# A one-core transformer layer with retrieved experts: the blocks of gate matrices are moved to the end of the first expert pass, the last eight activations stay on chip, gates are read back eight chunks at a time

## What is computed

```python
def peer_block(tok, wq, keys, u, v):
    p = tok.shape[0]
    qr = (tok @ wq).reshape(p, PEER_HEADS, 2, PEER_DQ // 2).astype(jnp.float32)
    s = jnp.einsum('phcd,hckd->phck', qr, keys.astype(jnp.float32))
    top_s, top_i = lax.top_k(s, PEER_TOPK)
    cand = top_s[:, :, 0, :, None] + top_s[:, :, 1, None, :]
    ids = top_i[:, :, 0, :, None] * N_KEYS + top_i[:, :, 1, None, :]
    best, j = lax.top_k(cand.reshape(p, PEER_HEADS, PEER_TOPK * PEER_TOPK), PEER_TOPK)
    eidx = jnp.take_along_axis(ids.reshape(p, PEER_HEADS, PEER_TOPK * PEER_TOPK), j, axis=-1)
    g = jax.nn.softmax(best, axis=-1)
    act = jax.nn.gelu(jnp.einsum('phkd,pd->phk', u[eidx], tok))
    return jnp.einsum('phk,phkd->pd', (g * act).astype(tok.dtype), v[eidx])
```

## Time and profile before

| | us |
|---|---|
| median of 3 runs | 1929.91 (1926.39 to 1932.4) |
| profiled execution, its own time | 1931.49 |
| its span (first to last instruction) | 1929.8 |
| PE busy in the span | 1827.1 (95%) |
| DVE busy in the span | 1566.1 (81%) |

### The profile page before, as it was taken

One profiled execution on the slowest core, in us unless ns is written; L12 is line 12 of the kernel. 1 busy time (PEld: TensorE's weight loads), 2 busy tenths in 40 slices (PEclk: granted clock), 3 DMA queues, 4 the chain that ended last, 5 costly groups with the idle time before them and its releaser, 6 DMA issues.

```text
span 1929.8 us, 34458 instructions
## 1 busy us (share of the span) xinstructions
PE 1827.1 (95%) x12531; PEld 1206.1 (62%) x12542; DVE 1566.1 (81%) x2939; ACT 860.4 (45%) x1310; POOL 1068.1 (55%) x671
## 2 busy tenths in 40 slices
PE   9999999999998989999978999998999999999996
PEld 7647777777777756566545666664555555555554
DVE  7975566455357589999979999995699999999997
ACT  6444446565445534333435666662333333333331
POOL 2732122222245748667688888888455555555551
PEclk9999999999999989999999999999999999999998
DMA  5732114223354545678799999999999999999993
GB/s 204 217 106 91 55 56 122 97 76 107 134 171 156 183 151 166 211 239 289 269 387 343 405 414 416 415 378 405 377 399 401 401 402 402 393 400 396 400 363 131
DMA packets 178077, 517.61 MB, mean 268 GB/s; under 512 B 19032, under 2 KB 61024, under 8 KB 177448
## 3 DMA queue, kind: packets, MB, share of 16 engines
q1 hardware_dynamic: 85280, 246.22, 35.3%
q0 software_dynamic: 55296, 201.35, 27.2%
q10 hardware_dynamic: 37384, 68.50, 9.8%
HBM read 458.55 MB, written 57.46 MB: 267 GB/s over the span
## 4 chain that ended last, share of the span: by engine, by line
PE 39%; DVE 26%; DMA 23%; issue 4%; POOL 4%; ACT 3%; ACTq 1%; SPq 0%; DVEq 0%; POOLq 0%
DMA raw<-in_v_units 21%; PE ps L1942 17%; PE ps L2061 10%; DVE rows L1699 4%; PE ps L1958 3%; DVE w_lo L1828 2%; POOL w_lo L601 2%; ACT w_hi L725 2%; DMA rows<-in_u_rows,rowi 2%; PE ps L2215 2%; POOL rows L627 1%; DVE accS L1848 1%; DVE hot L1808 1%; DVE hot_hi L1811 1%; PE ps L2195 1%
## 5 line engine op out<-in xcount | busy, mean ns | idle before, releaser
L601 POOL TENSOR_TENSOR w_lo<-raw,w_hi 128x1024 bf16<-128x1024 f32 x253 | 554.7, 2200 | 489.6 <-ACT w_hi L725 450.7
L725 ACT ACTIVATE w_hi<-raw 128x1024 bf16<-128x1024 f32 x381 | 400.2, 1053 | 452.1 <-DMA raw<-in_v_units 274.5
L660 POOL DMA_INDIRECT rows<-in_v_units,rowi x192 | 290.9, 1515 | 238.3 <-DVE accS L1848 190.0
L1942 PE MATMUL ps<-h_hi,w_hi 128*128 128x384 bf16 x1024 | 337.8, 330 | 17.7 <-ACT hb L1119 17.7
L2444 PE MATMUL ps<-W_hi,w_hi 128*128 128x384 bf16 x992 | 324.9, 327 | 21.4 <-DVE W_lo L1866 19.6
L1942 PE MATMUL ps<-h_lo,w_hi 128*128 128x384 bf16 x1024 | 337.6, 330 | 0.0
L1942 PE MATMUL ps<-h_hi,w_lo 128*128 128x384 bf16 x1024 | 337.3, 329 | 0.0
L2444 PE MATMUL ps<-W_hi,w_lo 128*128 128x384 bf16 x992 | 324.3, 327 | 0.0
L2444 PE MATMUL ps<-W_lo,w_hi 128*128 128x384 bf16 x992 | 324.2, 327 | 0.0
L1699 DVE CUSTOM_DVE_ANT_0 rows<-rows,ps 128x1024 f32<-128x1024 f32 x192 | 227.5, 1214 | 39.6 <-DMA rows<-in_u_rows,rowi 38.4
L627 POOL DMA_INDIRECT rows<-in_u_rows,rowi x192 | 201.7, 1051 | 98.0 <-DVE dots L1699 52.9
(11 more groups left out here) (469 smaller groups left out, 3415.1 us busy)
## 6 DMA issues: line engine op xcount, KB each, us to landing
raw<-in_u_units SPq DMA_DIRECT2D x128, 512.0 KB, 5.5
raw<-in_v_units SPq DMA_DIRECT2D x128, 512.0 KB, 12.3
raw<-in_units SPq DMA_DIRECT2D x123, 512.0 KB, 3.2
hd<-hb ACTq DMA_DIRECT2D x128, 192.0 KB, 6.2
Hb<-hd SPq DMA_DIRECT2D x32, 768.0 KB, 11.2
gd<-gsb ACTq DMA_DIRECT2D x48, 384.0 KB, 9.4
Gb<-gd SPq DMA_DIRECT2D x32, 576.0 KB, 8.4
gz<-stage ACTq DMA_DIRECT2D x24, 288.0 KB, 2.1
```

What stands on the lines that cost most here:

```text
L601: pool.tensor_tensor(w_lo[:, k % RING, :], raw[:, k % RAW, :], w_hi[:, k % RING, :], ALU.subtract).then_inc(lo_ready, 1)
L660: pool.indirect_dma_start(out=rows[:, (ND + n) % RG, :], out_offset=None, in_=table, in_offset=bass.IndirectOffsetOnAxis(ap=index, axis=0))\
L725: act.activation(w_hi[:, k % RING, :], raw[:, k % RAW, :], ACT.Copy).then_inc(hi_ready, 1)
L1942: last = pe.matmul(ps[:, bank + half, 0:n], w[:, slot, col:col + P], x(k)[:, half * n:(half + 1) * n], start=(k == 0 and w is w_hi and x i ...
```

## The change

- **Gate blocks** start at body 8 (`J_G` = 8) and end with the first half; no plain bodies follow.
- **Dots** move: 11 instead of 6 per `pairs_of`, and between its steps; 6 before the exponentials, 12 before the turned routes (74 in all before the first gate step, before it was 60). The other 118 all lie in the 48 gate steps, 2 or 3 in each; before, 2 in each (6 in one), and 32 after the last.
- **Last activations**: body 15 writes its GELU results straight into `Hb`, with no store and no read; the second half starts with those eight chunks and then takes chunks 0 to 119.
- **Gates by eights**: `Gb` holds 8 chunks; SP reads 1152 KB for every second group, in pieces of 1536 bytes instead of 768.
- **First group's `w_out`**: its eight tiles use eight PSUM banks instead of two, so PE no longer waits there for the residual add (`x2_ready`); three `w_lo` move from POOL to DVE (`low_a`); the load of the keys is issued earlier.
- Smaller: the copy into `share` goes (the normalising multiply writes it); `accS`, `eq3`, `Gb` and `Hb` lie elsewhere, so one wait of the first sum goes.

```diff
-J_G = 6
+J_G = 8
+LOW_A = {5: U_WQ + 2, 6: U_WQ + 4, 7: U_WQ + 6}
-DOTS_EARLY = 6
-DOTS_WAIT, DOTS_HELD = 24, 4
-X_TURN = 32
-DOTS_TWO = 4
+DOT_STEPS = (1, 2, 3, 4, 5, 6, 9, 12, 15, 16, 19)
+DOTS_EARLY = len(DOT_STEPS)
+DOTS_EXP, DOTS_WAIT = 6, 12
+X_TURN = 22
+GG = 2 * GRP
+LAST_ON = NCH - BODY
...
+DOTS_BEFORE = DOTS_WQ + NFT * DOTS_EARLY + DOTS_EXP + DOTS_WAIT
+def dots_until(i):
+    if i <= X_TURN:
+        return DOTS_BEFORE + (NST - DOTS_BEFORE) * i // X_TURN
+    return NST + NX * (i - X_TURN) // (N_STEP - X_TURN)
...
+            def load_group(g, pg, gates=None):
+                sp.wait_ge(w_mul, (g - 1) * GRP)
                 sp.dma_start(Hb[pg][:, :, :].rearrange("e c t -> e (c t)"),
-                             hd[bass.ds(g, 1)].rearrange("o e c t -> (o e) (c t)")).then_inc(gh_in[pg], 16)
+                             hd[bass.ds(g - 2, 1)].rearrange("o e c t -> (o e) (c t)")).then_inc(h_in[pg], 16)
+                if gates is not None:
+                    load_g(*gates)
...
+            for k in range(RAW):
+                load(a["v_units"][LAST_ON + k], (U_V + k) % RAW, False, U_V + k - RAW + 1)
+            sp.wait_ge(paired, 1)
             for b in range(2):
                 sp.wait_ge(b_written[b], NBK // 2 * PIECES * 16)
+            load_g(NCH // GG - 1, 0)
+            for k in range(RAW, BODY):
+                load(a["v_units"][LAST_ON + k], (U_V + k) % RAW, False, U_V + k - RAW + 1)
+            sp.wait_ge(unit_used, U_V)
+            load_g(0, 1)
...
-            def chunk(j, k, first=False):
+            def chunk(j, k, first=False, keep=False):
                 act.wait_ge(unit_used, j * BODY + (U_PEER + k + 1))
+                if keep:
+                    act.activation(Hb[k // GRP][:, k % GRP, :], ps[:, k % 2, 0:TD], ACT.Gelu_apprx_tanh).then_inc(gelu_done, 1)
+                    high_half(None, U_PEER + k, j * 32 + 16 * ((U_PEER + RING + k) // RAW + 1))
+                    return
...
-            for j in range(J_END, NCH // BODY - 1):
-                for k in range(BODY):
-                    chunk(j, k)
-            for k in range(BODY):
-                chunk(NCH // BODY - 1, k)
-                for p in FIRST_W.get(k, ()):
-                    w_high(2 * p, 2 * p)
             act.wait_ge(dot_done, ND)
             act.activation(acts[:, :], dots[:, :], ACT.Gelu_apprx_tanh).then_inc(acts_done, 1)
+            w_high(0, 0)
+            w_high(2, 2)
             w_high(GRP, GRP)
...
-                dve.tensor_tensor(xT[:, j, TD:T], ps[:, j % 2, 0:NA], xT[:, j, TD:T], ALU.add).then_inc(x2_ready, 1)
+                dve.tensor_tensor(xT[:, j, TD:T], ps[:, j, 0:NA], xT[:, j, TD:T], ALU.add).then_inc(x2_ready, 1)
...
+                if j in LOW_A:
+                    low_a(LOW_A[j])
...
-            for s in range(dots_until(N_STEP), ND):
-                dot(s)
...
-                if j >= 2:
-                    pe.wait_ge(x2_ready, j - 1)
```

More of the change, by code:

```diff
@@ L228, in row_chunk @@
     if d < NFT * DOTS_EARLY:
[L229 to L237, removed]
+        return 5 + d * 42 // (NFT * DOTS_EARLY)
+    if s - RG < DOTS_BEFORE:
+        return 48 + (d - NFT * DOTS_EARLY) * 2 // 3
+    i = min(x for x in range(N_STEP) if s - RG < dots_until(x + 1))
+    return J_G * BODY - 1 + i * BODY // G_BODY
 def acc_slot(j):
@@ L382, in program @@
         assert used[0] <= ACT_HI + 2 * KT * T * 2
-        accS = place("accS", ACT_HI, [P, D], F32)
         used[0] = ARENA
@@ L413, in program @@
         tripB = sb("tripB", [P, 3, TD], F32)
+        eq3 = place("eq3", used[0], [P, 2, TOPK, HP], BF16)
+        eq = sb("eq", [P, 2, TOPK, P], BF16)
+        iota16 = sb("iota16", [P, TOPK, P], BF16)
         pair = sb("pair", [P, 4, TD], BF16)
@@ L445, in program @@
         wb = [sb(f"wb{p}", [P, 2, TD], F32) for p in range(2)]
-        Gb = [sb(f"Gb{b}", [P, NBK, GRP, TBLK], F32) for b in range(2)]
-        Hb = [sb(f"Hb{b}", [P, GRP, TD], F32) for b in range(2)]
+        accS = sb("accS", [P, D], F32)
+        assert NBK * GG * TBLK * 4 <= 2 * KT * TD * 2 and 2 * KT * TD * 2 + GRP * TD * 4 <= 2 * KT * T * 2
+        assert FREED + (NBK * GG * TBLK + GRP * TD) * 4 <= FREED + 3 * TD * 4 + 2 * TOPK * P * 2 + TOPK * P * 2
         assert used[0] <= TOP
@@ L537, in _, with load_g @@
                     load(a["u_units"][i * RAW + k], (U_PEER + k) % RAW, False, i * RAW + (U_PEER + k - RAW + 1))
[L538 to L542, removed]
+            def load_g(s, b):
+                sp.dma_start(Gb[b][:, :, :, :].rearrange("e b c t -> e b (c t)"),
+                             gd[:, :, bass.ds(s * GG, GG), :].rearrange("b e c t -> e b (c t)")).then_inc(g_in[b], 16)
@@ L555, in _ @@
-            for b in range(2):
[L556 to L565, removed]
@@ L566, in _ @@
-            for b in range(2):
-                sp.wait_ge(h_written[b], 8 * NCH)
+            load_g(NCH // GG - 1, 0)
[3 more added lines that the diff above has]
+            load_g(0, 1)
+            for b in range(2):
+                sp.wait_ge(h_written[b], 8 * LAST_ON)
+            with sp.Fori(0, (NG - 4) // 4) as i:
+                for b in range(4):
+                    load_group(i * 4 + (2 + b), b % 2, (i * 2 + (1 + b // 2), b // 2) if b % 2 else None)
@@ L634, in _ @@
                 low_half(n, n)
-            with pool.Fori(1, U_OUT2 // RING) as i:
+            with pool.Fori(1, U_WQ // RING) as i:
                 for k in range(RING):
                     low_half(i * RING + k, k)
-            for n in range(U_OUT2 // RING * RING, U_PEER + RING):
+            for n in range(U_WQ // RING * RING, U_PEER + RING):
+                if n in LOW_A.values():
+                    continue
+                if n - 1 in LOW_A.values():
+                    pool.wait_ge(lo_ready, n)
                 low_half(n, n)
@@ L1043, in _ @@
                 high_unit(U_OUT + j + RING)
+                if j == 1:
+                    act.dma_start(keys[:, :, :], a["keysT"]).then_inc(keys_in, 16)
                 if j:
@@ L1135, in two_bodies @@
                     for k in range(BODY):
-                        chunk(it * 2 + (J_G + b), k)
+                        chunk(it * 2 + (J_G + b), k, keep=last and b == 1)
                         if first and b == 0 and k == 1:
@@ L1586, in _, with low_a @@
                 merged_low(j)
+            def low_a(n):
+                dve.wait_ge(hi_ready, n + 1)
+                dve.wait_ge(lo_ready, n)
+                dve.tensor_tensor(w_lo[:, n % RING, :], raw[:, n % RAW, :], w_hi[:, n % RING, :],
+                                  ALU.subtract).then_inc(lo_ready, 1)
             def out_low_a(k):
@@ L1757, in _ @@
                     pairs_of(i, NPH, top[:, i - 1, :, :], topi[:, i - 1, :, :], topf, abf, eq, iota16,
-                             tripB[:, :, (i - 2) * P:(i - 1) * P])
-                for x in range(DOTS_EARLY):
-                    dot(DOTS_WQ + (i - 1) * DOTS_EARLY + x)
+                             tripB[:, :, (i - 2) * P:(i - 1) * P], dot_beside)
             EARLY_DONE = DOTS_WQ + NFT * DOTS_EARLY
+            for x in range(DOTS_EXP):
+                dot(EARLY_DONE + x)
             NB_ = (NFT - 1) * NPH
@@ L2429, in _ @@
             two_bodies(NBLK // 2 - 1, last=True)
-            with pe.Fori(J_END, NCH // BODY) as j:
-                for k in range(BODY):
-                    chunk(j, k)
             pe.wait_ge(b_evac, N_STEP)
```

53 lines of the change are left out of this document (24 added, 29 removed).

## The result

| | before | after |
|---|---|---|
| median of 8 runs each, us | 1929.82 | 1938.16 (1935.55 to 1941.66) |
| ratio to before, 95% interval | | 1.0041 (1.0030 to 1.0052) |
| profiled execution, its own time | 1931.49 | 1938.19 |
| its span | 1929.8 | 1936.1 |
| PE busy in the span | 1827.1 (95%) | 1827.6 (94%) |

A forecast was written before the change was run, and what follows sets the result against it. PE, busy 95% of the span, was taken as the bound, with gains only where it waits or is clocked lower; -3.5 - 28.8 + 27.7 - 12.2 - 4 = -20.8 against 1931.5 gave 1910, range 1886 to 1937.

The forecast's parts named there:

- (e): Second half: larger pieces and fewer reads save, double gates' reads ahead of weights cost; -4 us, bounds -19.6 and +21.
- slower rival: Second half: the gates' double reads hold up the weights on SP; +21 us there, time 1935, some 1950 at worst; chance 0.14.
- (a): First group's `w_out`: eight banks and three `w_lo` moved to DVE shorten PE's waits; -3.5 us, bounds 0 and 7.1 gained.
- Larger pieces: Second half: gates read in pieces of 1536 bytes instead of 768 take back 8 us over the 128 chunks.
- two reads fewer: Second half: two reads of activations go, 1.6 MB at 401 GB/s, saving 3.9 us.
- (b): First gate steps: DVE's tiles come in time, so 21.8 us of waits and 7.0 of lower clock go; -28.8 us.
- (c): Settled gate bodies: more dots and fetches make six bodies 40.2 us and two 40.0; +27.7 us, bounds +10 and +47.
- (d): Hand-over to the second half: old waits and lower clock go, a 3.5 us wait at its start comes; net -12.2 us.
- DMA sum: Gate bodies: 16.6 MB a body at 413 GB/s takes 40.2 us in the six bodies that store a gate block.
- DVE sum: Gate bodies: 0.46 more dots a step make a DVE step 6.67 us instead of 6.11, a body 40.0.
- rival that clashes go: Gate bodies keep PE's pace: DVE's clashes with POOL go and DMA has slack; (c) is 0, time 1883; chance 0.17.
- a sign that I had named against it: Start of the second half: ACT waiting for units 4 to 7, queued on SP behind the first gates' read, would show the forecast wrong.

The follow-up runs named there:

- even: Changed kernel with half of the gates' read in each group instead of a double read every second group; 1917.72 us, ratio 0.9931 to before.
- fours: Changed kernel with gates read for four chunks in 768-byte pieces in each group, as before the change; 1919.84 us, ratio 0.9940 to before.
- half_load: Kernel even, with only half the bytes of each `u` unit loaded from chunk 80 on; 1897.02 us profiled.
- pool_low: Changed kernel with all `w_lo` of the first group's output made by POOL again, eight banks kept; 1934.17 us, ratio 1.0007 to before.
- even_pool: Kernel even, with all `w_lo` of the first group's output made by POOL again; 1912.66 us, ratio 0.9914 to before.

## Why the prediction was wrong

**The step that failed first is (e).** I had priced what every second group loses: 0.9 to 2.3 us more of DVE's waiting, "13 to 33 us over 14 of them". Then I wrote that "the queue is full either way, so what one group loses the next can give back", and took 8. That is what failed. A queue that is full on average is not full in each group: after the light group it runs low (0.82, 298 GB/s), and that time is gone. The loss was 20 us (525.8 against 505.5 with the even split), inside the bounds that I had worked out and then left; some 7 of it are the lower clock behind the waits, which I had not priced. It is the mechanism of my slower rival, at about its mild price: I had +21 for (e) and 1935, measured are +16.5 and 1938, with one long `W_lo` wait in every second group, 9 of 14 over 2 us, that I had named as its sign. That 1938 lies so near to 1935 is partly luck: it holds 7.6 us by which (a) missed. The Trainium skill ("DMA: Bandwidth & Descriptors", Queues, rings and completion order) says that descriptors are consumed in ring order on each engine; the 16 us of the weight that stands right behind the double read agree with that.

Larger pieces were to give back 8 us. Fours lies 2.1 us above even, not told apart from nothing, and both move 393 GB/s from 1400 to 1880 us. The profiled second half of fours is 5.1 us longer than that of even, but kernels with the even split spread there from 499.8 to 507.2 us, so a smaller gain is not excluded. By the rule of the Trainium skill ("DMA: Bandwidth & Descriptors", Specifications) that 512 bytes are enough for line rate, eights gain nothing. The runs agree with that as far as they can tell, and my comparison of two mixes did not hold. The 3.9 us for two reads fewer do not show either: fours takes 510.6 us where the kernel before takes 509.2.

**(a) had the wrong sign**: -3.5 taken, +4.1 in the traces. I counted three `w_lo` as 3.7 us of DVE's time and as clashes spared, and did not look where in DVE's order they stand: behind adds 5 to 7, while ACT makes the first of those `w_hi` by 597.1. Moved to 2, 4 and 6 the same instructions give about what I had forecast (112.7 to 115.7 against 117.5 before, -1.8 to -4.8). And "the 2.5 us for the residual add go" failed: the wait for the eighth add that replaced the old ones was in the code, I named no price for it, and it is where PE stood for 7.8 us, for 5.2 and 7.2 with POOL, and still for 3.2 to 3.5 with the early places.

**(b) was right**: 19.7 of 21.8 us of waits went, the clock is full, and the fourth gate tile of the first step was begun at 1040.8, where I had forecast all four by 1037 and PE's need at 1047; PE came to that step at 1052.9.

**(c) was right in its sum, for one of its two reasons.** Bodies took 36.7, 37.4, 41.2, 38.5, 40.0, 40.7, 39.7 and some 44.5 us (the last with the 3.9 us of (d) in it), 318.7 in all, so 314.8 without these, against 321.2. The DMA sum (40.2) is what binds. The DVE sum (40.0) is refuted by half_load: 118 dots fit into 36.7. The rival that clashes go was thus half right, but hidden by the bytes.

**(d) was right for PE**: the wait at the start of the second half is 3.9 us, forecast 3.5. But a sign that I had named against it did show: ACT waited for the first of the units 4 to 7, queued behind the first gates' read, and longer for the first unit behind the second one (timeline of ACT):

```profile
1348.09 1.06 ACT L738 ACTIVATE w_hi<-raw 128x1024 bf16<-128x1024 f32 x1 [3.37 <-DMA raw<-in_v_units]
1379.89 1.06 ACT L738 ACTIVATE w_hi<-raw 128x1024 bf16<-128x1024 f32 x1 [10.22 <-DMA raw<-in_v_units]
```

Little of it reached PE, which next waited for `W_lo` for 0.7 us, at 1385.8.

That the sum of (b), (c) and (d) fits so well (-12.4, forecast -13.3) is partly luck: (c) cost 21.3 us (314.8 against 293.5 at PE's own pace) where I had taken 27.7, so (b) and (d) together gave 33.7 where I had taken 41.0.

## What to carry to other kernels

Price a change of order by the queue that it stands in and group by group: a mean share of 1.03 promises nothing about the group behind which the queue runs dry, and a double read ahead of every second group's weights cost 20 us that went when it was split evenly or issued behind the weights. When work moves to another engine, ask when that engine gets to it, not only how long it takes there, and follow the buffer that it frees around the whole circle. When a wait is taken out, price the one that takes its place. To learn which of two full engines binds, take work from each in turn; a wait that ends on one of them says more than its busy share.

## What was unexpected of the hardware

- A full row is not a limit. In half_load DVE is busy 192.11 of 193.0 us, the DMA share is 1.03, and PE still waits for neither; with all bytes the same dots fit worse, because DVE then waits for its rows (`rows` <- DMA, 12.6 us in the changed kernel's 193). Part of DVE's busy time seems to be waiting inside its instructions: the same four tiles of a gate step take 4.07 us on average in the kernel before (1061 to 1276 us) and 3.57 in half_load.
- The clock may fall behind one and the same wait or not. pool_low and even_pool have the same code up to the mark and differ there by 4.6 us (114.6 and 119.2). Both have PE's wait of 1.74 us that ends at 589.8 or 589.9, but behind it the granted clock of pool_low stays at the higher level (2.4 GHz), while even_pool's is at the lower one (1.2 GHz) for 3.4 us, with 32 matmuls in 4 us instead of 51; and its next wait, for the eighth residual add, is longer (7.2 instead of 5.2 us). The windows, pool_low first:

```profile
591.00:595.00 4.00, 4.00 (x51) 4.00 (x49) 1.30 (x3) 2.75 (x5) 2.87 (x2) 1.00 0.49 142
```
```profile
591.00:595.00 4.00, 4.00 (x32) 3.81 (x30) 0.62 (x2) 1.67 (x2) 2.12 (x1) 0.57 0.21 83
```

So a single profile of a stretch with short waits can be some microseconds off, as the 112.7 to 115.7 us of equal code above also show.
